# Another table of expert shapes and their order, and the last block's rows kept on chip, in a diffusion layer with a 64-expert MoE

## What is computed

```
idx, gates = route(xf, w_router, router_bias)          # 8 experts for each token
def expert_block(args):
    tok, e = args
    xb = xpad[tok]
    hb = jax.nn.silu(xb @ w_gate[e]) * (xb @ w_up[e])   # 1024 -> 256
    return hb @ w_down[e]                               # 256 -> 1024
routed = segment_sum(rows * row_gate, row_tok)          # 8 rows a token
shared = (silu(xf @ ws_gate) * (xf @ ws_up)) @ ws_down
x = x + gate * (routed + shared);  y = rms_norm(x, norm_f)
```

## Time and profile before

| | us |
|---|---|
| median of 3 runs | 1075.47 |
| lowest, highest | 1075.21, 1076.78 |
| the profiled execution | 1077.48 |
| its span, first to last instruction | 1075.6 |
| PE busy | 1002.1 (93%) |
| DVE busy | 326.3 (30%) |
| ACT busy | 227.1 (21%) |
| POOL busy | 160.9 (15%) |
| chain that ended last: PE | 75% |
| chain that ended last: DMA | 15% |
| HBM read, written | 298.78 MB, 31.39 MB |

### The profile page before, as it was taken

The page is one execution under the profiler, slowest core; times in us unless marked ns, Lnnn a source line. Parts: engine busy times, 40 slices in busy tenths (PEclk is TensorE's granted clock), DMA queues, the critical chain, the costliest instruction groups (busy, mean ns, idle before and its releaser), DMA issues.

```text
span 1075.6 us, 17979 instructions
## 1 busy us (share of the span) xinstructions
PE 1002.1 (93%) x7100; PEld 449.5 (42%) x7100; DVE 326.3 (30%) x815; ACT 227.1 (21%) x537; POOL 160.9 (15%) x232
## 2 busy tenths in 40 slices
PE   6999999999999999999999999899898999899474
PEld 2655556565455554333443333333332343333121
DVE  0122226764236773111121111111111121111177
ACT  1211105664123231111121111111111121111011
POOL 1000010300221121211212211211111112110000
PEclk9999999999999999999999999999999999999798
DMA  9954419400400756699999999999999999994596
GB/s 371 406 238 173 157 31 247 165 1 1 176 40 31 270 213 241 230 387 405 390 421 422 420 420 420 421 419 416 421 418 414 408 420 421 419 416 186 236 410 261
DMA packets 59676, 321.64 MB, mean 299 GB/s; under 512 B 9748, under 2 KB 10396, under 8 KB 31560
## 3 DMA queue, kind: packets, MB, share of 16 engines
q1 hardware_dynamic: 43184, 272.71, 63.2%
q0 software_dynamic: 14240, 43.34, 10.3%
q10 hardware_dynamic: 2168, 4.43, 1.1%
HBM read 298.78 MB, written 31.39 MB: 307 GB/s over the span
## 4 chain that ended last, share of the span: by engine, by line
PE 75%; DMA 15%; DVE 5%; ACT 2%; issue 1%; SPq 1%; POOL 0%; POOLq 0%; DVEq 0%; ACTq 0%
PE bank L1977 27%; PE bank L1997 13%; PE bank L1571 8%; DMA ring<-in_w_up 8%; PE bank L1742 5%; PE bank L1949 3%; DMA ring<-expert_rows 3%; DMA reg_p<-in_w_up 3%; PE bank L1836 3%; PE bank L1598 2%; PE bank L1769 2%; PE bank L1560 2%; PE bank L1849 2%; PE bank L1755 1%; PE bank L1842 1%
## 5 line engine op out<-in xcount | busy, mean ns | idle before, releaser
L1977 PE MATMUL bank<-ring,reg_h 128*32 128x512 f32 x2528 | 330.9, 601 | 14.1 <-DMA ring<-in_w_up 12.3
L1977 PEld LDWEIGHTS bank<-ring,reg_h 128*32 128x32 f32 x2528 | 98.6, 111 | 200.3 <-issue 200.2
L1997 PE MATMUL bank<-ring,reg_y 128*32 128x512 f32 x1264 | 166.9, 594 | 1.5 <-ACT reg_y L997 1.5
L1977 PE MATMUL bank<-reg_p,reg_h 128*32 128x512 f32 x608 | 128.5, 601 | 2.0 <-DMA ring<-in_w_up 2.0
L1443 DVE TENSOR_TENSOR reg_h<-reg_p,bank 128x256 f32<-128x256 f32 x49 | 20.6, 421 | 342.3 <-ACT reg_p L1015 300.5
L707 POOL DMA_INDIRECT expert_rows<-reg_y,rowc x49 | 49.2, 1003 | 259.4 <-DVE reg_y L1427 258.1
L1015 ACT ACTIVATE reg_p<-bank 128x256 f32<-128x256 f32 x49 | 18.8, 383 | 327.2 <-PE bank L1977 327.2
L1571 PE MATMUL bank<-ring,reg_h 128*128 128x384 f32 (+2 forms) x256 | 84.3, 487 | 0.0
L1997 PEld LDWEIGHTS bank<-ring,reg_y 128*32 128x32 f32 x1264 | 46.2, 110 | 82.7 <-issue 78.7
L1427 DVE TENSOR_SCALAR reg_y<-bank,reg_p 128x512 f32<-128x512 f32 x49 | 36.8, 751 | 138.3 <-PE bank L1997 138.3
L1742 PE MATMUL bank<-ring,reg_h 128*128 128x512 f32 x160 | 70.3, 594 | 0.0
(11 more groups left out here) (272 smaller groups left out, 967.3 us busy)
## 6 DMA issues: line engine op xcount, KB each, us to landing
ring<-in_w_gate SPq DMA_DIRECT2D x51, 1024.0 KB, 15.2
ring<-in_w_up SPq DMA_DIRECT2D x51, 1024.0 KB, 21.4
ring<-in_w_down SPq DMA_DIRECT2D x51, 1024.0 KB, 20.0
ring<-in_w_mod SPq DMA_DIRECT2D x21, 1024.0 KB, 8.0
ring<-expert_rows SPq DMA_DIRECT2D x19, 1024.0 KB, 14.2
reg_p<-in_w_gate SPq DMA_DIRECT2D x13, 1024.0 KB, 14.0
reg_p<-in_w_up SPq DMA_DIRECT2D x13, 1024.0 KB, 22.8
reg_p<-in_w_down SPq DMA_DIRECT2D x13, 1024.0 KB, 21.9
```

The source lines that it names most:

```text
L1977: last = pe.matmul(bank[2 + p][R * j:R * j + R, :], xg_t[:, p, k * P + R * j:k * P + R * j + R], w_gu(homes[n % SLOTS])[:, k], start=(k == ...
L1997: last = pe.matmul(bank[5 + hf][R * j:R * j + R, :], h_t[:, p, i * P + R * j:i * P + R * j + R], w_dn(homes[n % SLOTS])[:, i, 512 * hf:512 ...
```

## The change

It has two parts.

**The table and the order.** `FIXED` is 1 in place of 2: expert 1 is ranked with the others and fetched only when the ranks are known (SP's early loads of n = 1 move behind the wait for `s_eid`). `UNITS` loses one expert of 4 tiles and one of 1, and has one more of 3 and one more of 2; the sum is 196 as before. `ORDER` now comes from a rule: at each place it picks the rank whose tiles bring the running total closest to a line that first runs up to 8 tiles behind the mean and later up to 6 tiles ahead of it.

**The last block.** Block 48 (`KEPT`) is not scattered. Its rows stay in `yb[:, 0]`. Since the rows in DRAM that it would have filled must count as nothing, POOL writes zeros there once, ahead of the first scatter. DVE makes for each token tile a 128 x 128 matrix of ones and zeros that says which row of the block belongs to which token (`kept_tokens`), and PE starts each tile's sum with two matmuls of that matrix by the kept rows. SP begins to fetch token rows when block 47 is through down and its scatter has landed; pieces 6 and 7 also wait for gate_up of block 48, and pieces from 8 on for its down. The ten buffers are taken in another order, the slots of block 48's experts last. Block 47's down goes to banks 0 and 1, and stands ahead of gate_up(48). The loop of extra blocks uses the odd buffers.

```diff
-FIXED = 2
-UNITS = (4,) * FIXED + (5,) * 5 + (4,) * 15 + (3,) * 20 + (2,) * 21 + (1,)
-ORDER = tuple(range(FIXED)) + tuple(FIXED + (i // 2 if i % 2 == 0 else E - FIXED - 1 - i // 2) for i in range(E - FIXED))
+FIXED = 1
+UNITS = (4,) * FIXED + (5,) * 5 + (4,) * 15 + (3,) * 21 + (2,) * 22
+EDGE, BEHIND, AHEAD = 8, 8, 6
+def expert_order():
+    left, total = list(range(FIXED, E)), 0
+    count, mean = len(left), sum(UNITS[FIXED:]) / len(left)
+    order = list(range(FIXED))
+    for n in range(1, count + 1):
+        x = n / count
+        due = mean * n - BEHIND * min(1, n / EDGE) * (1 - x) + AHEAD * x * min(1, (count - n) / EDGE)
+        r = min(left, key=lambda rank: (abs(total + UNITS[rank] - due), UNITS[rank]))
...
+ORDER = expert_order()
...
-            load_gate_up(1, 1)
-            load_down(1, 1)
             sp.wait_ge(s_eid, 1)
+            for n in (1, 2):
+                load_gate_up(n, e[n])
+                load_down(n, e[n])
...
-            sp.wait_ge(s_y, groups * 4 + NQ)
-            sp.wait_ge(s_yo[0], groups * 64 + 16 * n_even)
-            sp.wait_ge(s_yo[1], 16 * n_odd)
+            sp.wait_ge(s_y, KEPT)
+            sp.wait_ge(s_yo[0], 16 * n_even)
+            sp.wait_ge(s_yo[1], groups * 64 + 16 * n_odd)
             for n in range(4 * T):
+                if n == 6:
+                    sp.wait_ge(s_g, NQ)
+                if n == 8:
+                    sp.wait_ge(s_y, NQ)
...
+            pool.wait_ge(s_shx, T)
+            pool.wait_ge(s_tab, 1)
+            pool.memset(yb[:, 0, :], 0.0).then_inc(s_zero, 1)
+            pool.tensor_copy(rowc[:, 0:1], row_i[:, KEPT:KEPT + 1]).then_inc(s_idx, 1)
+            pool.indirect_dma_start(out=y_dram, out_offset=bass.IndirectOffsetOnAxis(ap=rowc[:, 0:1], axis=0),
...
             next_gather(2)
             next_gather(3)
...
-            next_scatter(NQ - 1)
...
+            def kept_tokens():
+                for t in range(T):
+                    last = dve.tensor_scalar(token_at[:, t:t + 1], tok_i[:, kept], float(-t * P), None, ALU.add)
+                link(last)
+                for t in range(T):
+                    last = dve.tensor_scalar(token_hit[:, t, :], iota, token_at[:, t:t + 1], None, ALU.is_equal)
+                last.then_inc(s_kept, 1)
...
             for b in range(0, NQ, 2):
                 if b:
                     block_down(b - 2)
+                if b == KEPT:
+                    block_down(b - 1)
                 block_gate_up(b)
-                if b:
+                if b and b < KEPT:
                     block_down(b - 1)
...
+            pe.wait_ge(s_kept, 1)
+            pe.wait_ge(s_ya, NQ)
+            pe.wait_ge(s_yb, NQ)
             for t in range(T):
+                for hf in range(2):
+                    pe.matmul(bank[2 * (t % 2) + hf][:, :], token_hit[:, t, :], yb[:, 0, 512 * hf:512 * hf + 512], start=True, stop=False)
```

More of the change, by code:

```diff
@@ L48 @@
 R = 32
-FIXED = 2
-UNITS = (4,) * FIXED + (5,) * 5 + (4,) * 15 + (3,) * 20 + (2,) * 21 + (1,)
-ORDER = tuple(range(FIXED)) + tuple(FIXED + (i // 2 if i % 2 == 0 else E - FIXED - 1 - i // 2) for i in range(E - FIXED))
+FIXED = 1
[9 more added lines that the diff above has]
+        r = min(left, key=lambda rank: (abs(total + UNITS[rank] - due), UNITS[rank]))
+        left.remove(r)
+        order.append(r)
+        total += UNITS[r]
+    return tuple(order)
+ORDER = expert_order()
 FIRST = tuple(sum(UNITS[r] for r in ORDER[:n]) for n in range(E))
@@ L466, in build @@
         PART = (0, 4, 2, 6)
+        ROWS_AT = tuple(slot(s) + 2048 * i for s in (0, 2, 3) for i in range(3)) + (slot(1),)
         def token_rows(n):
-            return view(ring, 2048 * (n % RBUF), 2, D)
+            return view(ring, ROWS_AT[n % RBUF], 2, D)
+        ROWS_BY = ((s_gu, 0), (s_gu, 1), (s_gu, 4), (s_dn, 0), (s_dn, 1), (s_dn, 4), (s_gu, 2), (s_gu, 3), (s_dn, 2), (s_dn, 3))
         def rows_in(n):
-            i = n % RBUF
-            s, each = (s_gu[i], 32) if i < SLOTS else (s_dn[i - SLOTS], 16)
-            return s, each * len(range(i % SLOTS, E, SLOTS)) + 16 * (n // RBUF + 1)
+            by, i = ROWS_BY[n % RBUF]
+            return by[i], (32 if by is s_gu else 16) * len(range(i, E, SLOTS)) + 16 * (n // RBUF + 1)
         def freed(n):
@@ L483, in freed, with scattered, y_banks @@
             return s_tp, 2 * t + j // 2 + 1
+        KEPT = NQ - 1
+        def scattered(b):
+            return 16 * (b // 2) + (16 if b % 2 == 0 else 0)
+        def y_banks(b):
+            return (0, 1) if b == KEPT - 1 else (5, 6)
         def xt_banks(b):
@@ L749, in _ @@
                         pool.sem_inc(s_pool, 1)
-                        pool.tensor_copy(tokc[:, 0:1], tok_i[:, bass.ds(b, 1)]).then_inc(s_idx, 1)
+                        pool.tensor_copy(tokc[:, 1:2], tok_i[:, bass.ds(b, 1)]).then_inc(s_idx, 1)
                         pool.wait_ge(s_idx, done + 1)
                         pool.sem_inc(s_pool, 1)
[L753 to L757, removed]
+                        gather(1)
+                        scatter(b, 1, done + 2, i * 64 + 16 * (n_odd + j))
+            pool.wait_ge(s_xg[0], 16 * n_even)
+            pool.wait_ge(s_xg[1], groups * 64 + 16 * n_odd)
         @block.scalar
@@ L1041, in _ @@
                         b = i * 4 + NQ + j
[L1042 to L1045, removed]
+                        xt_half(b, 1)
+                        silu(b, 1)
+                        h_t_out(b, 1)
+                        y_half(b, 1, i * 64 + 16 * (n_odd + j), gate_x)
             for t in range(T):
                 act.wait_ge(s_x3, t + 1)
-                act.activation(yb[:, 1, :], xs[:, t, :], ACT.Square,
+                act.activation(squared, xs[:, t, :], ACT.Square,
                                accum_out=ssq[:, 2 * T + t:2 * T + t + 1]).then_inc(s_ssq, 1)
@@ L2060, in _ @@
                             last = pe.matmul(bank[2 * (t % 2) + hf][:, :], ident, token_rows(n)[:, k, 512 * hf:512 * hf + 512],
-                                             start=(i == 0 and k == 0), stop=(i == 1 and k == 1))
+                                             start=False, stop=(i == 1 and k == 1))
                     last.then_inc(s_tp, 1)
```

66 lines of the change are left out of this document (41 added, 25 removed).

## The result

| | before | changed |
|---|---|---|
| median of 4 runs, us | 1076.12 | 1061.49 |
| lowest, highest | 1075.21, 1077.72 | 1061.13, 1063.04 |
| ratio, 95% interval | 1 | 0.9865 (0.9848 to 0.9882) |
| span of the profiled execution | 1075.6 | 1059.3 |
| gate_up(0) starts | 409.0 | 407.8 |

The change made the kernel 14.6 us faster; 29.5 us were forecast, and the time lies outside the range. The last two rows say where. The blocks became 6.8 us shorter (forecast: 18.8 less the 1.9 us of PE's new order, 16.9), the tail 8.3 us (forecast 12.4, to 61.5 us). The 1.2 us by which the first block starts sooner belong to the waits for `w_mod` ahead of it, 1.5 us in place of 2.8. So 10.1 us are missing in the blocks and 4.1 in the tail. These lengths come from one execution each, and a kernel's executions differ: the two profiled ones lie 16.4 us apart, the medians 14.6.

What follows compares the result with a forecast made beforehand. PE was taken to bound the blocks, with 22.8 us of lateness from late loads; 1077.48 - 18.8 (order) - 10.5 (last block) = 1048.2 us profiled, a median of 1046 us, range 1040 to 1058.

Steps and rivals of the forecast that it cites:

- the 1.9 us of PE's new order: End of the blocks: gate_up(48) has no down behind it to hide silu and product, so PE ends 1.9 us later.
- What bounds the kernel before: Blocks: PE bounds them, with 22.8 us of lateness, 16.2 waiting for up matrices and 6.6 of lost clock.
- The ledger, with "4 us left": Blocks: bytes needed at 419 GB/s against each block's start; the new order leaves 4 of 22.8 us, gaining 18.8.
- The bounds of that step: Lateness left in the blocks: between 0 and some 15 us, the latter at 394 GB/s up to block 17.
- a supply that is only fair: Rival: early loads come at only 394 GB/s, 1046 + 11 = 1057 us; chance 0.18.
- Early blocks: Blocks 5 to 9: margins thinnest, 0.4 to 1.0 us, so PE waits about 3 us there, once.
- The rival of starving at 343 GB/s: Early blocks: loads up to block 17 take 40.7 us longer at 343 GB/s, 1087 us; chance 0.06.
- POOL's gathers "hidden, by 0 to 3 us": Start: gathers of blocks 2 and 3 go at about 414 and 416, PE wants them at 423.3; no cost.
- The last block's fetch: Tail: SP issues the first token row fetch at 995.8, not 1006.53, 10.7 us earlier; gain taken as 10.5 us.
- DVE's way through its loop, 8.4 us,: Tail: DVE passes its 14 skipped iterations in 8.4 us after block 48, then sums with hardly a wait for pieces.
- the rival that SP is held by a semaphore or its loop: Tail: the first fetch does not move, 1056.5 us; chance 0.09.
- PE's first tile, "ten matmuls ... done" 6.7 us after its start,: Tail: PE's first tile is ten matmuls, done at 1019.2; DVE, ready at 1017.1, waits 2.1 us for it.

Runs made afterwards that it cites:

- edge4: `both` with EDGE, BEHIND, AHEAD = 4, 5, 6 in place of 8, 8, 6 in the expert order; 0.9719 of the kernel before, 1048.2 us.
- order_only: The kernel before with the new table and order of experts alone, without the last block's part; 0.9881 of the kernel before, 12.8 us faster.
- end_moved: `both` with one expert of five tiles moved in the order from place 60 to place 57; 0.9737 of the kernel before.
- pe_branch: The changed kernel with one condition around PE's loop of extra blocks alone, other engines' loops as before; 0.9827 of the kernel before.
- (zeros): The changed kernel with memset, copy and scatter of zeros moved behind the gathers of blocks 2 and 3; 0.9815 of the kernel before.
- (loops): The changed kernel with every engine's loop of 14 skipped iterations inside one condition; 0.9812 of the kernel before.
- (order): The step from `both` to `edge4`, fewer small experts close together in the order; 5.4 us better than `both`.
- both: The changed kernel with zeros written behind the gathers of blocks 2 and 3 and skipped loops inside one condition; 0.9769 of the kernel before.
- no_loop: The changed kernel with zeros written late and the loop of extra blocks left out on all engines; 0.9757 of the kernel before.

## Why the prediction was wrong

The forecast's mechanism is there, its size is not: 14.6 us of 29.5. Step by step:

- **What bounds the kernel before** held. The 22.8 us of lateness in its blocks is borne out by `edge4`: 592.7 - 22.8 + 1.9 = 571.8 us would be the blocks without a wait for a load, and it has 574.3 with 2.2 us of waits left.
- **The ledger, with "4 us left", failed**, and it is the largest miss. `order_only` leaves 22.8 - 10.5 = 12.3 us. The ledger adds bytes from 416.21 on at 419 GB/s and asks whether the sum is in by the time, and from a first stretch that just fits it concludes "whoever comes later has that much more room". That holds only while there is always a load to issue and the rate stays. (Of the changed kernel's 14.1 us over a run of blocks without a wait, 6.8 are waits for up matrices, 2.3 the gather, and most of the rest is clock behind them.) For block 45 (n = 59) the ledger's own formula gives 211.8 MB, ready at 921.6, against a start at 926.4: 4.8 us to spare. The load landed at 940.13, and PE, by then 11.8 us behind the ledger's start, still waited 2.10 us.

The step that failed is the constant 419 GB/s. From 415 to 940 us the changed kernel's DMA engines moved 407 GB/s: 349 up to 457, 421 up to 538, 413 up to 918 and 376 up to 940. At 407 the 211.8 MB are in at 936.6, and at 939.6 with the 3 us to land. For the last stretch the reason is in the loads. A load can't be issued before the slot of the fifth expert back is free. SP issued this one's second half at 916.55, when block 42's gate_up had freed the slot (911.7) and block 41's down had released SP (915.0); the next it could issue went at 927.93, behind block 42's down, and the one after at 934.93, behind block 44's gate_up. Just ahead of PE's wait the DMA engines are not full:

```profile
930.00:940.00 10.00, 8.16 (x78) 2.21 (x68) 1.17 (x2) 1.07 (x2) 0.91 (x3) 1.00 0.91 343
```

That does not explain the long middle: 413 GB/s at a share of 1.01, where the kernel before had 419 at the same share, is 5.4 us over 380, and no run here shows where it comes from. Nor does `end_moved` single out the slots, since by the ledger too it gives block 45 19.8 us to spare (n = 57, 205.5 MB). The formula does name the places. Redone for `edge4`, its least margins between blocks 20 and 46 are 6.6, 7.1 and 7.5 us at blocks 27, 31 and 35, and three of that kernel's four waits are there (0.31, 0.40, 0.29 us); the fourth, 1.20 us, is at block 47, with 8.7. What it lacks is a rate that holds.
- **The bounds of that step**, 0 to 15 us, did hold the 12.3. The value inside was taken from "a queue that ran empty", which was right for 457 to 538 us (421 GB/s for 394), half right for 416 to 457 (356 for 259), and said nothing on the rest. No rival named the measured time; the nearest, a supply that is only fair (1057 us), has the right quantity, the rate, at another time.
- **Early blocks**: waits of about 3 us at blocks 5 to 9, once. They were at 5, 8 and 13, 4.7 us, and 3 us of clock at 13 (10.04 for 7.07), in the first profile; in the second 3.2 us at 5, 9 and 13 and no clock there. The rival of starving at 343 GB/s did not come.
- **POOL's gathers "hidden, by 0 to 3 us" failed.** The times of issue were right; the landing was taken from a lone scatter's 3.21 us, while a gather issued behind weights took 9.74. The trace before had the price in its list of DMA issues, all 49 gathers and all 49 scatters with the median us from issue to landing:

```profile
reg_h<-h_rows,tokc POOLq DMA_INDIRECT x49, 9.5
expert_rows<-reg_y,rowc POOLq DMA_INDIRECT x49, 9.3
```

A gather issued at 416 is then there at about 425.5, against 423.3 when PE wants it; PE waited 2.30 us. By the ratios it cost 5.4 us, with 2.5 us either way by the two intervals, and 3.4 in the profiles' blocks.
- **The last block's fetch** came as worked out, 7.75 us ahead of the read of y(48) (1003.6 - 995.8 = 7.8 in the forecast); PE's 1.9 us were 2.0 (waits of 1.02 and 0.95).
- **DVE's way through its loop, 8.4 us,** was 8.5, and the rival that SP is held by a semaphore or its loop did not come.
- **PE's first tile, "ten matmuls ... done" 6.7 us after its start, failed.** The row it was taken from the earlier trace rows names eight entries for one piece of two rows; a tile has two pieces, 16 entries, and four for the kept rows. It took 10.75 us (1002.84 to 1013.6), of which 8.6 are the tile at full clock and the rest the half clock at its head, and DVE waited 6.50 us in place of 2.1. That is the tail's 4.1 us. `pe_branch` gets as much back in another way, by an earlier start of the tile, which still takes as long: 61.7 us against 61.5 forecast. The two extra matmuls take 1.72 us a tile, not 0.9; with them a tile costs PE 8.60 us, just under DVE's 8.90, so this costs nothing yet.

The three failures met one at a time: 5.4 (zeros) + 5.7 (loops) + 5.4 (order) = 16.5 us by the ratios, or 15.7 from the changed kernel to `edge4`, for a shortfall of 15.5. Only the first is an error undone; the single condition and the other order go beyond the kernel that was forecast, so this shows that the time was lost in these three places, not what each wrong step cost to a microsecond. The kernel with all three is at 0.9719, which is 1045.9 us on this scale; 1046 was forecast. That it agrees to 0.1 us is luck: the interval of this ratio alone is 2 us to either side.

The rule of the Trainium skill that spoke against the change (DMA: Bandwidth & Descriptors, "Where 436 GB/s comes from", 358 GB/s) is not borne out after either: 421 GB/s over 81 us in the stretches above.

## What to carry to other kernels

Where loads go through a few slots, a sum of bytes against a deadline tells where it is tight but gives only the earliest time: follow single loads, from the event that frees the slot to the work that needs it, above all where small pieces of work stand together. A transfer's time from a row where the queue was empty is no price for one that is issued behind others; take the median of its kind under load. When a span with slack loses that slack, count again everything that had hidden in it, the record counts of a row and the engine's clock after a pause included.

## What was not expected of the hardware

- A loop of 14 iterations that does nothing held DVE for 7.8 us and PE for 9.2, some 0.6 us an iteration. The Trainium skill (Advanced Engine Details and Errata, "Control Flow Timing") gives about 108 ns for a compare-and-branch; 14 of these would be 1.5 us. No run here shows what the rest is.
- A single condition that is not met still held PE for 3.4 to 5.0 us (3.4, 4.0, 4.2, 4.4, 5.0 in five kernels) and DVE for 0.49 us. In a sixth, `edge4`, the first of the four entries behind it came after 0.97 us and PE then stood 2.49 us ahead of the second. With the code absent it was 0.97, a wait for DVE. That the jump is over PE's far longer code is a guess; its length was not varied, and in `edge4` the pause stands behind the first entry that follows the jump.
- What a pause costs in clock differs. PE's four kept-row entries took 3.78 us after 9.2 us of standing and 3.75 after 4.2 to 5.0 (granted clock 0.50 in all), 3.64 and 3.19 after 3.4 and 4.0 (0.55 and 0.65), and 1.95 after 0.97 (1.00). But a wait of 3.0 to 3.3 us for a load at block 5 left that gate_up at 7.07 us in three kernels (`both`, `end_moved`, `no_loop`), one of 3.45 made it 8.77 and 9.81 in two others, and one of 2.84 at block 13 made it 10.04. No rule by the pause's length comes out of these.
